# Two-layer decoder trunk: the memory values of all cross heads in one projection, a reordered cross step, and first output tiles that take their last input at the end

## The reference, cut to what matters

```python
mh = rms_norm(mem, mem_norm_w[i])                       # 256 x 1024
mk, mv = jnp.split(mh @ w_mem_kv[i], 2, axis=-1)        # 256 x 512 each
mk = mk.reshape(b, m_len, CROSS_HEADS, CROSS_HEAD_DIM)  # 4 heads of 128
mv = mv.reshape(b, m_len, CROSS_HEADS, CROSS_HEAD_DIM)
xq = xq.reshape(b, s, CROSS_HEADS, CROSS_HEAD_DIM)
sc = jnp.einsum('bqhd,bkhd->bhqk', xq, mk).astype(jnp.float32) * (CROSS_HEAD_DIM ** -0.5)
pc = jax.nn.softmax(sc, axis=-1).astype(mv.dtype)
co = jnp.einsum('bhqk,bkhd->bqhd', pc, mv)
y_c = co.reshape(b, s, CROSS_WIDTH) @ w_o_cross[i]
...
x = x + (g_a * y_a + g_b * y_b + g_c * y_c) @ w_out[i]
```

## Time and profile before

| what | value |
|---|---|
| median of three runs (lowest, highest) | 2023.81 us (2023.42, 2023.92) |
| the profiled execution: its own time | 2023.66 us |
| its span, first to last instruction | 2021.8 us |
| mean granted TensorE clock | 0.997 |
| ScalarE, VectorE, GpSimd busy | 44%, 51%, 54% |

### The profile page before, as it was taken

How to read it: one execution, slowest core, us unless ns; L and a number is a source line. 1 busy time by engine, 2 the same in 40 slices (tenths; PEclk the granted TensorE clock), 3 DMA queues, 4 the chain that set the end, 5 groups by cost and what they waited for, 6 DMA issues and landing times.

```text
span 2021.8 us, 29003 instructions
## 1 busy us (share of the span) xinstructions
PE 1988.0 (98%) x9357; PEld 1635.9 (81%) x9357; DVE 1023.1 (51%) x1767; ACT 884.6 (44%) x1548; POOL 1083.4 (54%) x1424
## 2 busy tenths in 40 slices
PE   6999999999999999999999999999999999999997
PEld 5888788888888888888888788878878888888886
DVE  6445777776754433321134657777766543333211
ACT  6434555555634332233344445555564432322332
POOL 6556344444465555557764644444436555555673
PEclk9999999999999999999999999999999999999999
DMA  6333223223553333333353332322245423333232
GB/s 219 104 112 105 73 75 88 84 68 94 193 161 99 94 96 101 93 113 92 99 167 92 101 94 83 83 69 83 82 133 187 133 87 102 96 102 91 86 93 84
DMA packets 358545, 213.01 MB, mean 105 GB/s; under 512 B 15478, under 2 KB 343228, under 8 KB 357692
## 3 DMA queue, kind: packets, MB, share of 16 engines
q1 hardware_dynamic: 342462, 173.87, 30.1%
q10 hardware_dynamic: 15998, 38.04, 5.3%
HBM read 191.40 MB, written 20.45 MB: 105 GB/s over the span
## 4 chain that ended last, share of the span: by engine, by line
issue 40%; POOL 38%; PE 20%; POOLq 1%; ACT 0%; DMA 0%; DVE 0%; SPq 0%; ACTq 0%; DVEq 0%
POOL w_lo L549 38%; PE proj L587 7%; PE proj L588 7%; PE proj L589 7%; POOLq L554 0%; POOLq L552 0%; DMA raw<-in_w_out 0%; PE flip L969 0%; ACT y_out L1468 0%; POOL rope_t L540 0%; PE score L988 0%; PE score L599 0%; POOL freq L523 0%; POOLq L549 0%; DVE x_sum L1627 0%
## 5 line engine op out<-in xcount | busy, mean ns | idle before, releaser
L549 POOL TENSOR_TENSOR w_lo<-raw,w_hi 128x256 fp32r<-128x256 f32 x1376 | 1077.7, 815 | 914.8 <-ACT w_hi L1006 913.8
L587 PE MATMUL proj<-h_hi,w_hi 128*128 128x512 f32 (+1 forms) x1616 | 645.2, 399 | 0.0
L589 PE MATMUL proj<-h_hi,w_lo 128*128 128x512 f32 (+1 forms) x1616 | 630.6, 390 | 0.0
L588 PE MATMUL proj<-h_lo,w_hi 128*128 128x512 f32 (+1 forms) x1616 | 629.9, 390 | 0.0
L1006 ACT ACTIVATE w_hi<-raw 128x1024 fp32r<-128x1024 f32 x344 | 362.8, 1056 | 207.0 <-DMA raw<-in_w_down 58.5
L587 PEld LDWEIGHTS proj<-h_hi,w_hi 128*128 128x128 f32 (+1 forms) x1616 | 303.6, 188 | 64.7 <-issue 4.4
L588 PEld LDWEIGHTS proj<-h_lo,w_hi 128*128 128x128 f32 (+1 forms) x1616 | 303.6, 188 | 64.6 <-issue 3.8
L589 PEld LDWEIGHTS proj<-h_hi,w_lo 128*128 128x128 f32 (+1 forms) x1616 | 303.2, 188 | 64.8
L587 PE MATMUL proj<-hid_hi,w_hi 128*128 128x512 f32 x352 | 137.6, 391 | 0.0
L589 PE MATMUL proj<-hid_hi,w_lo 128*128 128x512 f32 x352 | 137.1, 389 | 0.0
L588 PE MATMUL proj<-hid_lo,w_hi 128*128 128x512 f32 x352 | 137.0, 389 | 0.0
(11 more groups left out here) (384 smaller groups left out, 3015.0 us busy)
## 6 DMA issues: line engine op xcount, KB each, us to landing
raw<-in_w_in SPq DMA_DIRECT2D x232, 256.0 KB, 3.1
raw<-in_w_gate_up SPq DMA_DIRECT2D x176, 256.0 KB, 3.0
raw<-in_w_down SPq DMA_DIRECT2D x96, 192.0 KB, 2.5
gate_in<-gate_scratch ACTq DMA_DIRECT2D x48, 256.0 KB, 3.4
gate_scratch<-gate_out ACTq DMA_DIRECT2D x46, 256.0 KB, 2.0
raw<-in_w_mem_kv SPq DMA_DIRECT2D x32, 256.0 KB, 2.9
raw<-in_w_o_diff SPq DMA_DIRECT2D x32, 256.0 KB, 3.0
raw<-in_w_out SPq DMA_DIRECT2D x32, 256.0 KB, 2.9
```

Of the source, the lines that this page charges most:

```text
L549: ins = g.tensor_tensor(w_lo[s][:, cols], raw[s % 2][:, cols], w_hi[s][:, cols].bitcast(F32), ALU.subtract)
L587: mm(o, hi[:, c:c + width], rh, start=start and k == 0, stop=False)
L588: mm(o, hi[:, c:c + width], rl, start=False, stop=False)
L589: ins = mm(o, lo[:, c:c + width], rh, start=False, stop=stop and k == n - 1)
```

## The change

The memory values of all four heads are projected at once in stage N. Now the normalised memory (`mem_hi`, `mem_lo`) is the stationary operand, and 512 columns of weights move. The result has memory rows on partitions, in two banks, so the transposes of the values fall away, and so does `vT` here. Stage N gets four slots for it (4 to 7), each of two pieces of 128 channels by 512 columns; a cross step has three slots instead of four. In a cross step the latent tile comes ahead of attend. The loops over cross steps are written out. In layer 0 the bank that the key tile needs is copied first. In stage F, tiles 0 and 1 take seven mix tiles each, and then both the eighth. The diff, cut to its core:

```diff
+        cv_hi = at("cv_hi", T + 20 * KB, [P, NM, SEQ], F32R)
+        cv_lo = at("cv_lo", T + 24 * KB, [P, NM, SEQ], F32R)
...
+        MEM_ORDER = (2, 0, 1, 3)
-        SLOTS = dict(N=(5, 1), C=(4, CROSS - 1), A=(6, 1), ...
+        SLOTS = dict(N=(8, 1), C=(3, CROSS - 1), A=(6, 1), ...
-        FLIPS = dict(C=(4, CROSS), B=(7, HEADS))
+        FLIPS = dict(C=(2, CROSS), B=(7, HEADS))
...
sync engine
                 slot(l, "N", 0, 3, *whole(w_mem_kv, l, 0))
-                slot(l, "N", 0, 4, *whole(w_mem_kv, l, 512))
-                with sp.Fori(0, CROSS - 1) as i:
+                for s in range(4):
+                    slot(l, "N", 0, 4 + s, (0, tiles(w_mem_kv, l, 2 * s, 2 * s + 1, 512, 512)), (512, tiles(w_mem_kv, l, 2 * s + 1, 2 * s + 2, 512, 512)))
+                for i in range(CROSS - 1):
                     cross_slots(l, i)
...
TensorE
+            def memory_values(l):
+                pe.wait_ge(flip_read.sem, flip_read.at(l, "C"))
+                for s in range(4):
+                    w = ring("N", 4 + s)
+                    pe.wait_ge(slot_lo.sem, slot_lo.at(l, "N", 0, 5 + s))
+                    for n in range(2):
+                        k, c = 2 * s + n, slice(512 * n, 512 * n + 512)
+                        for t in range(NM):
+                            o, m = flip[t][:, :], slice(t * P, (t + 1) * P)
+                            mm(o, mem_hi[:, k, m], w_hi[w][:, c], start=k == 0, stop=False)
+                            mm(o, mem_hi[:, k, m], w_lo[w][:, c], start=False, stop=False)
+                            ins = mm(o, mem_lo[:, k, m], w_hi[w][:, c], start=False, stop=k == KD - 1)
+                    ins.then_inc(slot_done.sem, 1)
...
-                    pe.wait_ge(mem_copied, KD // 2)
+                    pe.wait_ge(mem_copied, 1)
                 project_mem(l, "N", 0, 3, att, (att_read, att_read.at(l, "C")))
-                project_mem(l, "N", 0, 4, score[0], (exp_done, exp_done.at(l, "C")))
+                memory_values(l)
                 pe.wait_ge(gate_copied.sem, gate_copied.at(l, "N", 0, 1))
-                flip_memory(l, 0)
...
-                with pe.Fori(0, CROSS - 1) as i:
+                for i in range(CROSS - 1):
                     cross_scores(l, i)
                     project_xq(l, i)
                     project_mem(l, "C", i, 1, 1, (tile_ready, tile_ready.at(l, "C", i + 1)))
                     cross_flip(l, i)
-                    project_mem(l, "C", i, 2, 0, (xq_copied, xq_copied.at(l, "C", i + 1, 1)))
+                    project_cq(l, i)
                     cross_attend(l, i)
-                    project_cq(l, i)
-                    flip_memory(l, i + 1)
...
+                for e in range(2):
+                    unit(l, "F", 0, e, e, (tile_ready, tile_ready.at(l, "F")), KD - 1, mix_rhs, before=mixed, stop=False)
+                for e in range(2):
+                    unit(l, "F", 0, e, e, None, 1, lambda k: mix_rhs(KD - 1), first=(KD - 1) * P, before=lambda k: mixed(KD - 1),
+                         start=False).then_inc(slot_done.sem, 1)
+                for tile in range(2, KD):
+                    jj, e = tile // 4, tile % 4
+                    unit(l, "F", jj, e, e % 2, (tile_ready, tile_ready.at(l, "F", jj, e - 1)), KD, mix_rhs).then_inc(slot_done.sem, 1)
...
ScalarE
+            def memory_values_high(l):
+                act.wait_ge(slot_done.sem, slot_done.at(l, "N", 0, 8))
+                for t in range(NM):
+                    copy(cv_hi[:, t, :], flip[t][:, :]).then_inc(cv_high.sem, 1)
...
                 out_cross(l, "N", 0, 3, att, kT[:, 0:MEM], MEM)
-                act.wait_ge(mem_stored, 16)
-                out_cross(l, "N", 0, 4, score[0], vT[:, 0:MEM], MEM)
-                split_ahead(l, "N", 0, 4)
-                memory_high(l, 0)
+                for s in range(4, 8):
+                    split_ahead(l, "N", 0, s)
+                memory_values_high(l)
...
-                with act.Fori(0, CROSS - 1) as i:
+                for i in range(CROSS - 1):
                     cross_step(l, i)
-                    split_ahead(l, "C", i, 0)
-                    split_ahead(l, "C", i, 1)
+                    split_ahead(l, "C", i, 0, i)
+                    split_ahead(l, "C", i, 1, i)
                     out_cross(l, "C", i, 1, proj[1], kT[:, 0:MEM], MEM)
                     cross_high(l, i)
-                    split_ahead(l, "C", i, 2)
-                    out_cross(l, "C", i, 2, proj[0], vT[:, 0:MEM], MEM)
-                    split_ahead(l, "C", i, 3)
-                    squares(l, "C", i + 1, 0, cq_raw[:, bass.ds(i + 1, 1), :].rearrange("p a n -> p (a n)"))
-                    memory_high(l, i + 1)
+                    split_ahead(l, "C", i, 2, i)
+                    squares(l, "C", i + 1, 0, cq_raw[:, i + 1, :])
+                act.wait_ge(mem_stored, 16)
...
VectorE
+            def memory_values_low(l):
+                for t in range(NM):
+                    ve.wait_ge(cv_high.sem, cv_high.at(l, "N", 0, t + 1))
+                    v.tensor_tensor(cv_lo[:, t, :], flip[t][:, :], cv_hi[:, t, :].bitcast(F32), ALU.subtract).then_inc(cv_split.sem, 1)
...
                 if l == 0:
                     rope_rows()
-                memory_low(l, 0)
+                memory_values_low(l)
...
-                with ve.Fori(0, CROSS - 1) as i:
+                for i in range(CROSS - 1):
                     begin(l, "C", i)
                     cross_prob(l, i)
                     out_xq(l, "C", i)
                     cross_low(l, i)
+                    out_cq(l, i + 1, "C", i, 2)
                     cross_out(l, i)
-                    out_cq(l, i + 1, "C", i, 3)
-                    memory_low(l, i + 1)
                     end("C")
```

More of the change, by code:

```diff
@@ L407, in slot @@
                 assert len(parts) == 2
-                half = ring(stage, s, step if stage == "B" else 0) % 2
+                half = ring(stage, s, step if stage in "BC" else 0) % 2
                 for col, src in parts:
@@ L426, in cross_slots @@
                 slot(l, "C", i, 1, *whole(w_mem_kv, l, i * P + P))
-                slot(l, "C", i, 2, *whole(w_mem_kv, l, i * P + (512 + P)))
-                slot(l, "C", i, 3, *whole(w_in, l, i * P + (C_CQ + P)))
+                slot(l, "C", i, 2, *whole(w_in, l, i * P + (C_CQ + P)))
             def two_tiles(l, col):
@@ L790, in cross_attend @@
             def cross_attend(l, i):
-                pe.wait_ge(flip_read.sem, flip_read.at(l, "C", i, 4))
+                pe.wait_ge(flip_read.sem, flip_read.at(l, "C", i, 2))
                 pe.wait_ge(att_read.sem, att_read.at(l, "C", i))
-                product([(att[:, :], v_hi[:, j, :], v_lo[:, j, :], pt_hi[:, j * SEQ:(j + 1) * SEQ], pt_lo[:, j * SEQ:(j + 1) * SEQ])
+                c = slice(i * P, (i + 1) * P)
+                product([(att[:, :], cv_hi[:, j, c], cv_lo[:, j, c], pt_hi[:, j * SEQ:(j + 1) * SEQ], pt_lo[:, j * SEQ:(j + 1) * SEQ])
@@ L802, in project_xq @@
             def project_xq(l, i):
-                unit(l, "C", i, 0, 0, (kv_copied, kv_copied.at(l, "C", i + 1)), KD, h_rhs).then_inc(slot_done.sem, 1)
+                unit(l, "C", i, 0, 0, (xq_copied, xq_copied.at(l, "C", i, 1)), KD, h_rhs, w=ring("C", 0, i)).then_inc(slot_done.sem, 1)
             def project_mem(l, stage, step, s, b, free):
-                unit(l, stage, step, s, b, free, KD, lambda k: (mem_hi[:, k, :], mem_lo[:, k, :]), cols=MEM).then_inc(slot_done.sem, 1)
+                unit(l, stage, step, s, b, free, KD, lambda k: (mem_hi[:, k, :], mem_lo[:, k, :]), cols=MEM, w=ring(stage, s, step)).then_inc(slot_done.sem, 1)
@@ L929, in _, with mixed, mix_rhs @@
                              lambda k: (outs_hi[:, k, :], outs_lo[:, k, :]), before=split).then_inc(slot_done.sem, 1)
[L931 to L940 removed]
+                def mixed(k):
+                    pe.wait_ge(mix_split.sem, mix_split.at(l, "E", 0, k + 1))
+                def mix_rhs(k):
+                    return mix_hi[:, k, :], mix_lo[:, k, :]
+                pe.wait_ge(ssq_read.sem, ssq_read.at(l, "B", HEADS))
+                pe.wait_ge(gate_copied.sem, gate_copied.at(l, "L", 0, 5))
+                for e in range(2):
[6 more added lines that the diff above has]
+                    unit(l, "F", jj, e, e % 2, (tile_ready, tile_ready.at(l, "F", jj, e - 1)), KD, mix_rhs).then_inc(slot_done.sem, 1)
                 unit(l, "G", 0, 0, 0, (tile_ready, tile_ready.at(l, "F", 1, 3)), KD, h_rhs,
@@ L1223, in cross_high @@
                 for j in range(NM):
-                    flip_high(l, "C", i, 2 + j, pt_hi[:, j * SEQ:(j + 1) * SEQ], flip[j][:, :])
-            def memory_high(l, i):
-                act.wait_ge(att_full.sem, att_full.at(l, "C", i))
-                for j in range(NM):
-                    flip_high(l, "C", i, j, v_hi[:, j, :], flip[j][:, 0:P])
+                    flip_high(l, "C", i, j, pt_hi[:, j * SEQ:(j + 1) * SEQ], flip[j][:, :])
+            def memory_values_high(l):
```

(18 more changed lines are left out.)

43 lines of the change are left out of this document (16 added, 27 removed).

## The result

The changed kernel takes 2028.54 us (median of 9 runs, 2027.8 to 2030.23) against 2023.59 for the kernel before (9 runs, 2022.97 to 2024.75). The ratio is 1.0026, with a 95% interval of 1.0015 to 1.0036: 0.26% slower, a little beyond the 0.2% that a measurement can tell from no change. The forecast was 2027.0; the result lies in the range, and in case A's own (2025 to 2029.5), though just on the slower side of the limit. The new waits of case A are what the trace shows, in both layers; the half clock behind them, which case A put in both, stands in layer 1 only. The profiled execution took 2028.5 us with a span of 2026.7, 4.9 more than before. Among the runs of experiment 5's kernel is one of 7127.86 us, and among those of the kernel before that were taken beside experiments 5, 7 and 8 one of 8683.71; the ratios leave them out.

A forecast was written before the change was run, and what follows sets the result against it. TensorE, busy 98% of the span, was taken as the bound. Layer 1 +1.1, layer 0 -0.5, output tiles -0.5 and half clock +3.2 gave +3.3 on 2023.66: 2027.0 us, range 2016.5 to 2031.

The forecast's parts named there:

- case A: The forecast itself: new TensorE waits for p_a and half clock behind them in both layers, 2027.0 us; chance 0.42.
- Part 1: Values' matmuls on TensorE: 192 narrow ones replaced by 96 wide ones, counted by starts, gain 1.2 us.
- Part 2: Values' flips: transposes worth 1.7 us go, with layer 0's 2.2 us wait before them and 1.6 us of half clock.
- Part 3: First softmax: values' copies queue behind slot 10's load; flip waits 3.5 and 3 us; net +1.1 layer 1, -0.5 layer 0.
- The clock's term: Half clock on TensorE behind the new waits: 1.6 us in each layer, 3.2 together; bounds nothing or 1.6 each.
- Part 4: Order of a cross step: latent tile ahead of attend covers the probabilities' split; priced at nothing.
- Part 5: First output tiles: mix_lo wait goes (0.65 a layer), new 0.4 wait for tile 0's bank; -0.5 us for two layers.
- C: Rival: values' copies not held up, slot 10 arrives before the queue matters; 2017.4 us, chance 0.18.
- B: Rival: the waits come, but the clock holds in one or both layers; 2023.8 to 2025.4 us, chance 0.20.
- D: Rival: loads from slot 6 to slot 10 land in 4.2 us instead of 3.0; 2031.8 us, chance 0.14.
- E: Rival: grouped mean matmul durations are real prices, 17 us less for the values' matmuls; 2001 us, chance 0.03.
- F: Rival: the change partly fails, memory tiles still bound by something beside columns, no wait; 2023.8 us, chance 0.03.

The follow-up runs named there:

- experiment 5: Changed kernel, ScalarE's values' copies moved behind slot 5's split, and kT (step 0 also pt_hi) ahead of each cross step's second split: 2019.21 us, ratio 0.998.
- experiment 7: Changed kernel with attend before the next step's latent tile in each cross step, on TensorE and VectorE: 2043.3 us.
- experiment 8: Kernel of experiment 5 with, in layer 0, slot 6's split ahead of the row rms and the memory rows' store behind the values' copies: 2022.05 us, ratio 0.9991.
- experiment 4: Kernel before, with every 512-column matmul of the output tiles cut into two of 256 columns: 2028.71 us.
- experiment 9: Experiment 5's kernel, step 0's exponentials between slots 6 and 7's splits; layer 0: early slot 6 split, store behind step 0's pt copies: 2016.87 us, ratio 0.9968.
- experiment 2: The changed kernel run once more, unaltered: 2029.14 us.
- experiment 6: Changed kernel with only kT (step 0 also pt_hi) moved ahead of each cross step's second split, values' copies left behind slot 7's: 2028.15 us, ratio 1.0023.
- experiment 1: Changed kernel with ScalarE's two copies of the values moved ahead of the splits of slots 6 and 7: 2029.39 us, ratio 1.0028.
- experiment 3: Kernel before, with only the new order of the first two output tiles (seven eighths each, then their last eighth): 2022.74 us.

## Why the prediction was right, and where it was off

**Part 1 right.** The values' starts are 0.23 us apart in the trace after; experiment 4 measures the price of an additional matmul at 13 ns, against some 14 from the rows.

**Part 2 right in what it removed**: no flip of values and no wait before it. That the half clock behind that wait was worth 1.6 us holds for the profiled execution before; in experiment 4 the same stretch ran at full clock.

**Part 3 right to half a microsecond.** Slot 10's cast was forecast to begin at 1053.5 and began at 1053.36. The flips were forecast at 1061.6 and 69.0, and came at 1061.74 and 69.54. Since layer 1 began 0.33 us earlier than before, that is 0.5 later than forecast within the stage; layer 0's, whose start was 0.30 later, 0.2. The waits of 3.5 and 3 us were 3.00 and 3.49. One statement was wrong without effect on the time: "slot 7 is ready at 1045.0, so none starves". Its first matmul started at 1045.66 after a wait of 0.58 us, which came off the wait for p_a. In layer 0 the slots' own pauses (1.66 and 1.75 us) are those forecast with "slot 7 is ready at 53.15": its first matmul started at 52.93.

**The clock's term fits by luck.** I put 1.6 us behind the new wait in each layer. In the profiled execution it was nothing in layer 0 and 2.9 us in layer 1; in a second execution of the same kernel both layers fell. The sum happened to fit (3.2 against 2.9). How much it varies can be read from one stretch, from the first flip of p_a to the sum of squares. Where the clock held, it takes 454.75 us in layer 0 (454.76 in experiment 5) and, without the wait for pt_lo, 452.63 us in layer 1 (experiment 5; 452.64 in experiment 8, 452.60 in experiment 9). What it has over that is the price of the half clock:

| pause for p_a | layer 0: pause, price (us) | layer 1: pause, price (us) |
|---|---|---|
| the changed kernel | 3.49, 0.0 | 3.00, 2.9 |
| experiment 2 | 4.04, 1.6 | 3.30, 1.4 |
| experiment 6 | 3.60, 2.5 | 3.43, 1.6 |
| experiment 8 | 3.32, 1.6 | no pause |

The mean of the seven is 1.65, so 1.6 was a fair mean though it came from one stretch behind a pause of 2.2 us; the bounds "nothing or 1.6" were too narrow above.

**Part 4 right**: the changed kernel has no wait for pt_lo in its cross steps, and experiment 7 shows 14.8 us lost without the new order of attend and latent tile, 9.4 of them in such waits.

**Part 5 right in mechanism.** The mix_lo waits went, waits of 0.31 us (forecast 0.4) stand before tile 2, and the layers gained 0.3 and 0.4 us where I had 0.25 each.

**Not foreseen**: a wait of 0.85 us for a pt_lo in the last head of layer 1. All eight traces with the new cross stage (seven kernels) show it, at 0.5 to 1.1 us, and none of the three with the old one does. The traces say where it comes from. Ahead of it ScalarE issues six loads of gates (the ACTq row), and the copies to pt_hi, from which this pt_lo is made, stand behind them in its queue. In layer 0, and in layer 1 of the three kernels with the old stage, the six issues take 2.77 to 2.79 us; in layer 1 of the changed kernel they take 3.63, 0.86 more, and TensorE waits 0.85. In experiments 1, 2 and 5 to 9 the issues take 0.47 to 1.12 us longer, and each wait agrees with that to 0.02 us.

```profile
1498.78 2.77 ACTq L1033 DMA_DIRECT2D gate_in<-gate_scratch  x6
...
1502.80 3.63 ACTq L1056 DMA_DIRECT2D gate_in<-gate_scratch  x6
...
1512.12 0.55 PE L641 MATMUL flip<-ident,p_b 128*128 128x128 f32 x3 [0.85 <-DVE pt_lo L1567]
```

(The first line is from the kernel before.) Why the issues take longer was not tried and stays open. From the forecast +3.3 to the measured +4.9 it goes by this wait (+0.85), the flips later by 0.2 and 0.5, the ends of the span that no part of the change touches (+0.75), and against that the clock (-0.3) and the tiles (-0.2); that sum is 5.1, 0.2 off.

**The rivals.** C ("the values' copies are not held up", 2017.4) had the right size for a kernel whose needed copies are free, but its condition was wrong. I made it depend on the loads coming sooner, and on one copy. Experiments 1, 6 and 5 show that it depends on the order of the queue, and on two copies. With both freed, at unchanged loads, 2019.2 and then 2016.9 were reached. What the profiled execution of experiment 5 (2018.7) lacks to C's 2017.4 is about its wait for pt_lo (1.1 us) and for slot 7 in layer 1 (0.3 us), neither of which C has. The explanation that I carried into experiment 1 (one held copy) would have been taken for shown had I not run it. B (the clock holds in one or both layers) has its condition met in layer 0 of the profiled execution, but not its time, since layer 1 alone paid 2.9 us. D (slow loads) did not happen: layer 1's chain came within 0.2 us of the time from 3.0 us landings. E fell with experiment 4. F (no wait, and nothing gained) did not happen: the waits are there.

## What to carry to other kernels

When an engine that works strictly in order both casts incoming weights and copies results, a cast far ahead is a hidden wait for a load: go through its queue and ask of every copy, "which load must have landed before this runs?" Freeing one such copy shows nothing while the next stands behind the next load; free all of them on the path before judging the change, and let stores run where only casts with slack stand behind. Removing work from a 98% busy engine gains only what its feeders can follow: here the change with its 112 matmuls fewer cost 5 us, and the same work with one engine's queue in another order ran 7 us faster than the kernel before.

## What the runs showed of the hardware that I had not expected

The half clock behind an idle stretch is not a fixed price. Of eleven pauses of TensorE of 2.6 to 4.1 us ahead of p_a or kT in these traces, ten were followed by half clock (means of 0.50 to 0.73 in a window of 4 us), and one (3.49 us, layer 0 of the changed kernel) was not, while another execution of the same kernel fell there. Shorter pauses do not exclude it: of three of 2.2 us ahead of the old memory flip in layer 0 (the kernel before, experiments 3 and 4) two were followed by it, and of ten of 1.62 to 1.80 us for values' slots one (0.60 in 46 to 50 us, experiment 2). Where it fell behind such a pause it cost 1.4 to 3.1 us by the stretches worked out above, at the most as much as the wait itself (3.1 behind the 2.99 us for kT in experiment 1), and in experiment 7, where a second pause follows closely, 4.0 and 3.3. The Trainium skill (TensorE: Matmul & The Clock Gate, "What's actually happening") says that activity releases the throttle; the trace agrees in so far as the clock rose again while TensorE worked without a pause, at 1068 us in the rows of the changed kernel.

The starts of matmuls with the operands of this kernel are 120 ns apart at 256 columns and 227 at 512 (the kernel before, the changed one, experiment 4), so that two narrow ones take 13 ns more than one wide one. And the store of the memory's rows, issued in 0.33 us, goes with a DMA share near 1 for 4 us (293 and 368 GB/s in the windows of experiments 8 and 9), and the casts of the slots loaded beside it waited 5.57 and 5.16 us.
